# Forgetting attention with two buffer sets per head pair, and the next pair's projections placed among the score steps

## What is computed

```python
def fox_mixer(h, b_f):
    q, k, v, f_logit = jnp.split(h, [MIX_WIDTH, 2 * MIX_WIDTH, 3 * MIX_WIDTH], axis=-1)
    log_f = jax.nn.log_sigmoid((f_logit + b_f).astype(F32))
    decay = jnp.cumsum(log_f, axis=1).transpose(0, 2, 1)
    o = causal_block_attention(split_heads(q, 12), split_heads(k, 12), split_heads(v, 12), decay)
    return merge_heads(o)
# causal_block_attention, for s <= t:
#   logit[t,s] = q_t.k_s/sqrt(dk) + decay[t] - decay[s];  softmax over s;  times v
for i in range(DEPTH):                      # DEPTH = 4, kinds 0, 1, 2, 0
    x = layer_norm(ALPHA * x + 0.5 * swiglu(x, ...), ...)
    h = x @ w_in                            # for kind 0: q | k | v | forget logits | memory q
    main = fox_mixer(h[..., :-MEM_WIDTH], fox_b_f[j])
    mem_out = memory_attention(h[..., -MEM_WIDTH:], mem, mem_w_kv[i])
    x = layer_norm(ALPHA * x + jnp.concatenate([main, mem_out], -1) @ w_o[i], ...)
    x = layer_norm(ALPHA * x + 0.5 * swiglu(x, ...), ...)
```

## Time and profile before

| | us |
|---|---|
| median of six runs | 7801.82 (7759.95 to 8189.87) |
| the profiled run | 7766.0 |
| its span on the slowest core, core 7 | 7764.5 |
| PE busy | 6061.5 (78% of the span) |
| DVE busy | 3044.7 (39%) |
| ACT busy | 1837.7 (24%) |
| Pool busy | 923.9 (12%) |

### The profile page before, as it was taken

How to read it: one execution, slowest core, us unless ns; L and a number is a source line. 1 busy time by engine, 2 the same in 40 slices (tenths; PEclk the granted TensorE clock), 3 DMA queues, 4 the chain that set the end, 5 groups by cost and what they waited for, 6 DMA issues and landing times.

```text
span 7764.5 us, 85500 instructions; the slowest of 8 cores (7712.3 to 7764.5 us)
## 1 busy us (share of the span) xinstructions
PE 6061.5 (78%) x29076; PEld 2816.6 (36%) x29076; DVE 3044.7 (39%) x3788; ACT 1837.7 (24%) x3124; POOL 923.9 (12%) x1426
## 2 busy tenths in 40 slices
PE   7885887789888658898895466659989966885996
PEld 3342443344434223344442133324434432442442
DVE  1326555422322664223226266661321336555132
ACT  1211443211221102112212033321211213442121
POOL 1110111011111000111110011101111110110110
PEclk9996998999999679999996688889999987888998
DMA  7651001466665114656651200017666540110765
GB/s 125 90 77 12 10 10 21 64 92 80 85 93 78 17 16 63 91 77 90 93 79 13 24 7 6 11 19 94 86 92 87 71 60 7 12 15 14 95 87 103
DMA packets 671506, 440.05 MB, mean 57 GB/s; under 512 B 115024, under 2 KB 659792, under 8 KB 671056
## 3 DMA queue, kind: packets, MB, share of 16 engines
q0 software_dynamic: 649024, 401.02, 40.0%
q1 hardware_dynamic: 22064, 33.57, 1.4%
HBM read 826.51 MB, written 8.39 MB: 108 GB/s over the span
## 4 chain that ended last, share of the span: by engine, by line
PE 52%; DVE 16%; ACT 11%; DMA 10%; issue 7%; POOL 2%; DVEq 0%; ACTq 0%; POOLq 0%; SPq 0%
PE ps L220 51%; ACT arena L232 7%; DMA arena<-ffn_w_down 6%; DVE arena L486 3%; DVE st L256 2%; ACT xres L232 2%; PE ps L224 2%; DVE xres L267 2%; DVE xres L277 2%; POOL arena L465 2%; ACT L232 1%; DMA arena<-ffn_w_gate 1%; DMA arena<-w_o 1%; DVE xres L269 1%; ACT rstd L232 1%
## 5 line engine op out<-in xcount | busy, mean ns | idle before, releaser
L220 PE MATMUL ps<-arena 128*128 128x512 bf16 (+7 forms) x24992 | 5710.3, 379 | 1243.4 <-DVE xres L277 195.4
L220 PEld LDWEIGHTS ps<-arena 128*128 128x128 bf16 (+3 forms) x24992 | 2375.8, 101 | 4161.2 <-issue 2038.7
L232 ACT ACTIVATE arena<-ps 128x512 bf16<-128x512 f32 (+4 forms) x2612 | 1389.5, 566 | 3199.1 <-PE ps L220 3048.3
L385 DVE SCALAR_TENSOR_TENSOR arena<-arena,ps 128x512 bf16<-128x512 f32 x704 | 479.8, 687 | 1777.2 <-PE ps L220 1729.2
L486 DVE RECIPROCAL arena<-ps 64x512 f32<-64x512 f32 x208 | 699.0, 3361 | 565.9 <-PE ps L220 558.9
L277 DVE SCALAR_TENSOR_TENSOR xres<-xres,ps 128x512 f32<-128x512 f32 x384 | 246.3, 683 | 1188.4 <-PE ps L220 1178.0
L232 ACT ACT_TABLE_LOAD x107 | 137.3, 1283 | 1796.4 <-DVE mv L258 1584.5
L217 POOL DMA_DIRECT2D arena<-ffn_w_down x384 | 283.6, 740 | 1345.7 <-PE ps L220 1216.3
L224 PE MATMUL ps<-ident,xres 128*128 128x128 f32 x1536 | 218.5, 309 | 271.8 <-ACT arena L232 138.8
L465 POOL TENSOR_TENSOR arena<-arena,tri 128x128 bf16<-128x128 bf16 x576 | 237.1, 425 | 1577.0 <-ACT arena L232 1574.2
L220 PE MATMUL ps<-ident,tri 128*128 128x256 bf16 x2272 | 412.8, 266 | 0.0
(11 more groups left out here) (79 smaller groups left out, 812.4 us busy)
## 6 DMA issues: line engine op xcount, KB each, us to landing
arena<-ffn_w_down POOLq DMA_DIRECT2D x320, 512.0 KB, 6.8
arena<-ffn_w_gate POOLq DMA_DIRECT2D x176, 512.0 KB, 5.8
arena<-ffn_w_up POOLq DMA_DIRECT2D x176, 512.0 KB, 5.8
arena<-ffn_w_down POOLq DMA_DIRECT2D x64, 256.0 KB, 5.2
arena<-fox_w_in POOLq DMA_DIRECT2D x40, 256.0 KB, 5.3
xres<-x SPq DMA_DIRECT2D x4, 2048.0 KB, 27.4
out<-xres SPq DMA_DIRECT2D x4, 2048.0 KB, 9.1
gb<-ln_g SPq DMA_DIRECT2D x12, 512.0 KB, 4.1
```

The lines of the kernel that those rows point to most:

```text
L220: return sc.emit("pe", lambda e: e.matmul(out, lhsT, rhs, start=start, stop=stop), reads, writes, signal=signal)
L232: return sc.emit("act", lambda e: e.activation(out=out, in_=in_, func=func, **kw), reads, writes)
L385: vop(lambda e, fc=fc, bu=bu, th=th: e.scalar_tensor_tensor(out=aT[:, fc, th * 512:(th + 1) * 512], in0=sil[th][:, :], scalar=0.5, in1=psu ...
```

## The change

The buffers of q, k (with their decay and constant rows) and v exist twice, for even and odd pairs. The loads and projections of a pair become a list of 13 items: one that issues the three weight loads and the twelve decay-row transfers, four q groups, four k groups, four v groups. Pair 0's items run at once as before. For pairs 1 to 5 the list is handed to the attention of the pair before as a `Filler`: at every score step that had a dummy pair, the filler is asked, and on every fifth such step one item is issued in the dummy pair's place. What is left at the end of the second head is flushed there.

To make room, the decay buffer now lies over the odd v buffer, the memory attention's k and v over the even one; the three bf16 decay rows are stacked on partitions 0, 32 and 64 of `pc2`, which takes two further casts into a scratch `ptmp`; the constant rows are set in both buffer sets (eight memsets instead of four, two Pool memsets of v instead of one). The other mixers only get a renamed buffer for the memory attention's q.

```diff
+        class Filler:
+            def __call__(self):
+                self.n += 1
+                if self.items and self.n % self.pace == 0:
+                    self.items.pop(0)()
+                    return True
+                return False
+            def flush(self):
+                while self.items:
+                    self.items.pop(0)()
...
-                    if DUMMY_N and c0 == 0:
+                    did = False
+                    if filler is not None and c0 == 0:
+                        did = filler()
+                    if DUMMY_N and c0 == 0 and not did:
...
+            qa = [[carve(35968 + (2 * p + k) * 2048, 2048, BF16) for k in range(2)] for p in range(2)]
+            ka = [[carve(44160 + (2 * p + k) * 2048, 2048, BF16) for k in range(2)] for p in range(2)]
+            Vaug = [carve(52352 + p * 4096, 4096, BF16, "p (i s e) -> p i s e", i=16, s=2) for p in range(2)]
+            pc2 = carve(63104, 2048, BF16)
+            dec = carve(56448, 4096, F32)
...
             for r in range(3):
-                vop(lambda e, r=r: e.tensor_copy(out=pc[0:12, r, :], in_=dec[0:12, :]), ["dec"], ["pc"])
+                vop(lambda e, r=r: e.tensor_copy(out=pc2[32 * r:32 * r + 12, :], in_=dec[0:12, :]), ["dec"], ["pc"])
                 if r < 2:
+                    vop(lambda e: e.tensor_copy(out=ptmp[0:12, :], in_=dec[0:12, :]), ["dec"], ["ptmp"])
...
+            for p in range(2):
+                for s2 in range(2):
+                    vop(lambda e, p=p, s2=s2: e.memset(qa[p][s2][64:70, :], 1.0), [], [("qa", p, s2)])
+                    vop(lambda e, p=p, s2=s2: e.memset(ka[p][s2][64:70, :], -1.0), [], [("ka", p, s2)])
+                vop(lambda e, p=p: e.memset(Vaug[p][:, :, :, 64:128], 1.0), [], [("Vaug", p)], eng="pool")
...
+            def prep_items(hp):
+                p = hp % 2
+                items = []
+                def loads():
+                    dma("pool", wq[:, :, :], w_in_v[:, :, hp * 128:(hp + 1) * 128], [], ["wq"])
...
+                for tb in range(4):
+                    items.append(proj_item(wq, "wq", qa, "qa", 0.125, tb))
+                for tb in range(4):
+                    items.append(proj_item(wk, "wk", ka, "ka", None, tb))
...
+                for q4 in range(4):
+                    items.append(v_item(q4))
+                return items
+            for it in prep_items(0):
+                it()
             for hp in range(6):
+                fill = Filler(prep_items(hp + 1), 5) if hp + 1 < 6 else None
...
-                    attn_core(qa[s2], ("qa", s2), 0, ka[s2], ("ka", s2), 0, 70,
+                    attn_core(qa[p][s2], ("qa", p, s2), 0, ka[p][s2], ("ka", p, s2), 0, 70,
...
+                if fill is not None:
+                    fill.flush()
```

More of the change, by code:

```diff
@@ L193, in build_program @@
         onesb = sb("onesb", [128, 128], BF16)
-        ARENA = 63488
+        ARENA = 65536
         arena = sb("arena", [128, ARENA], BF16)
@@ L433, in build_program, with __init__ @@
         deferred_norm = []
+        class Filler:
+            def __init__(self, items, pace):
+                self.items = list(items)
+                self.pace = pace
+                self.n = 0
+            def __call__(self):
[7 more added lines that the diff above has]
+                    self.items.pop(0)()
         def flush_norm():
@@ new lines, in fox_phase @@
+            ka = [[carve(44160 + (2 * p + k) * 2048, 2048, BF16) for k in range(2)] for p in range(2)]
+            Vaug = [carve(52352 + p * 4096, 4096, BF16, "p (i s e) -> p i s e", i=16, s=2) for p in range(2)]
+            A["PT"] = [carve(60544 + k * 512, 512, BF16) for k in range(3)]
+            A["rec"] = carve(62080, 1024, F32)
+            pc2 = carve(63104, 2048, BF16)
+            dec = carve(56448, 4096, F32)
+            A["kmT"] = carve(52352, 512, BF16, "p (h m) -> p h m", h=2)
@@ L585, in fox_phase @@
             for r in range(3):
-                vop(lambda e, r=r: e.tensor_copy(out=pc[0:12, r, :], in_=dec[0:12, :]), ["dec"], ["pc"])
+                vop(lambda e, r=r: e.tensor_copy(out=pc2[32 * r:32 * r + 12, :], in_=dec[0:12, :]), ["dec"], ["pc"])
                 if r < 2:
-                    vop(lambda e, r=r: e.tensor_tensor(out=dec[0:12, :], in0=dec[0:12, :], in1=pc[0:12, r, :],
-                                                       op=ALU.subtract), ["dec", "pc"], ["dec"])
-            for s2 in range(2):
-                vop(lambda e, s2=s2: e.memset(qa[s2][64:70, :], 1.0), [], [("qa", s2)])
-                vop(lambda e, s2=s2: e.memset(ka[s2][64:70, :], -1.0), [], [("ka", s2)])
@@ new lines, in prep_items, with proj_item, f, v_item @@
+            def prep_items(hp):
[3 more added lines that the diff above has]
+                    dma("pool", wq[:, :, :], w_in_v[:, :, hp * 128:(hp + 1) * 128], [], ["wq"])
+                    dma("pool", wk[:, :, :], w_in_v[:, :, 768 + hp * 128:768 + (hp + 1) * 128], [], ["wk"])
+                    dma("pool", wv[:, :, :], w_in_v[:, :, 1536 + hp * 128:1536 + (hp + 1) * 128], [], ["wv"])
+                    for s2 in range(2):
+                        h = 2 * hp + s2
+                        for r in range(3):
+                            dma("sp", qa[p][s2][64 + r:65 + r, :], pc2[32 * r + h:32 * r + h + 1, :], ["pc"], [("qa", p, s2)])
+                            dma("sp", ka[p][s2][67 + r:68 + r, :], pc2[32 * r + h:32 * r + h + 1, :], ["pc"], [("ka", p, s2)])
+                items.append(loads)
+                def proj_item(w, wkey, dst, dkey, scale, tb):
+                    def f():
+                        b = 5 + (tb % 2)
+                        for c in range(8):
+                            mm(psum[b][:, :], w[:, c, :], xT[:, c, tb * 512:(tb + 1) * 512], c == 0, c == 7,
+                               [wkey, ("xT", c, tb)], [PK(b)], signal=(c == 7))
+                        for s2 in range(2):
+                            dve_copy(dst[p][s2][0:64, tb * 512:(tb + 1) * 512], psum[b][s2 * 64:(s2 + 1) * 64, :], [PK(b)],
+                                     [(dkey, p, s2)], scale=scale)
+                    return f
+                for tb in range(4):
+                    items.append(proj_item(wq, "wq", qa, "qa", 0.125, tb))
+                for tb in range(4):
+                    items.append(proj_item(wk, "wk", ka, "ka", None, tb))
+                def v_item(q4):
+                    def f():
+                        b = 5 + (q4 % 2)
+                        for tl in range(4):
+                            i = 4 * q4 + tl
+                            for c in range(8):
+                                mm(psum[b][:, tl * 128:(tl + 1) * 128], xT[:, c, i * 128:(i + 1) * 128], wv[:, c, :],
+                                   c == 0, c == 7, ["wv", ("xT", c, q4)], [PK(b)], signal=(c == 7 and tl == 3))
+                        dve_copy(Vaug[p][:, 4 * q4:4 * q4 + 4, :, 0:64],
+                                 psum[b][:, :].rearrange("p (i s e) -> p i s e", i=4, s=2), [PK(b)], [("Vaug", p)])
+                    return f
+                for q4 in range(4):
+                    items.append(v_item(q4))
+                return items
@@ L616, in fox_phase @@
[L616 to L619 removed]
+                    attn_core(qa[p][s2], ("qa", p, s2), 0, ka[p][s2], ("ka", p, s2), 0, 70,
+                              lambda kb, p=p, s2=s2: Vaug[p][:, kb, s2, :], ("Vaug", p), lambda tb: 4 * tb + 4, True,
                               lambda tb, h=h: mixT[(h % 2) * 64:(h % 2) * 64 + 64, h // 2, tb * 512:(tb + 1) * 512],
[L621 removed]
+                              lambda tb, h=h: ("mixT", h // 2, tb), A["PT"], A["rec"], filler=fill)
```

78 lines of the change are left out of this document (25 added, 53 removed).

## The result

The changed kernel takes 0.9917 of the time before, with a 95% interval of 0.9882 to 0.9951: 0.5% to 1.2% faster, on both sides of the 1% that the prediction took as its bound. Its profiled run took 7702.7 us, the one before 7766.0; 7694 was predicted, in a range of 7655 to 7765.

What follows compares the result with a forecast made beforehand. PE was taken to bound the attention's long runs of score steps. Removed stages -282.7, items and border waits +197 and set-up +13.6 gave -72 us: 7766 - 72 = 7694 us, range 7655 to 7765.

Steps and rivals of the forecast that it cites:

- Removed: Ten stages between head pairs, five a layer, in which ACT does nothing, disappear: 282.7 us together.
- Items: Projection pieces between attention score steps add to PE's queue almost in full: q and k 12.5 us a pair, v 3.2.
- The refilling rival: After each item the score, exp, PV chain refills at 0.59 us, 59 us for 100 items: 7753 us; chance 0.14.
- the case counted with it: Inside the attention, items wait on DVE's copies through shared banks, so the old stage returns; counted within refilling's 0.14.
- Set-up: Ahead of pair 0, extra DVE casts and memsets delay PE's start by 6.8 us a layer, 13.6 in all.
- The border wait: Between pairs, the first PV waits for the last v copy, queued behind DVE's last normalisation: 0.6 us a pair.
- I leave dips as they are: Dips to 1.2 GHz inside the attention follow waits around the small first block and were taken as unchanged.
- Two signs of being wrong: Granted clock in the pairs leaving 0.89 to 0.94; the stretch of a query block growing by more than its items.
- Little else: For projections between score steps, the change saves the load wait, the cold start, some dummies and little else.
- The greater gain: In the attention, a denser queue ends the clock dips, 17 us and 20 more: 7657 us; chance 0.17.
- The slower case: In the ten filled attention stretches, dips grow; granted share 0.84 uses up the gain, 0.75 gives 7873 us; chance 0.07.
- the Trainium skill's limiter: Three cores of a die on dense matmuls drop to 13/16 clock; the change would lose about 80 us.

## Why the prediction was right

Its sum was -282.7 + 197 + 13.6 = -72; the stretches give -69, the profiled run -63, the ratio -38 to -92. The bounds that it names add up to 7674 to 7735, not to 7670 to 7730.

*Removed.* 5 x 28.4 = 142.0 us a layer, as its 282.7 for both.

*Items.* In the first head five items stand (load, four q), predicted at 4 x 1.56 - 0.16 = 6.1 us; pair 0, which has no border ahead of it, grew by 5.8 there. In the second head stand four k and two v items, predicted 9.5; pairs 1 to 4 grew by 9.3 (pair 0, 8.4). The flush is 3.5 where 3.6 was predicted. The refilling rival would have added 0.59 us an item, 9 us for the first head, and is out. So is the case counted with it, that items wait for DVE's copies. PE's waits over the attention of layer 0, core 5 (before, on core 7: 54.7 us for Pool and 21.9 for weights):

```profile
PE ps L220 <- POOL arena L485: 56.7, 86, 1.7
PE ps L220 <- ACT arena L232: 1.1, 1, 1.1
```

Here too the five border waits are put down to Pool. For weights PE waited twice in the whole kernel, at pair 0 of each layer, 53.5 us together, as the view of this tensor says:

```profile
who waited for it (us, times):
  PE ps L220: 53.5, 2
```

*Set-up.* 6.7 us a layer for 6.8 predicted. From the start of the set-up the first q copy comes 53.8 us later (predicted 779.1 - 724.9 = 54.2, by the row of before above), PE's restart 55.4 us (55.7), the first q groups 44.8 us (45.3).

*The border wait, the step that was mis-sized.* Predicted 0.6 us a pair. The wait itself grew by 0.71. But the first head of pairs 1 to 4 grew by 7.2 us where the items make 6.1, and that of pair 5, which has no items at all, by 1.9: a border costs 1.1 to 1.9 us. What was left out stands behind "I leave dips as they are". Before, PE ran at 1.2 GHz for 92.8 us of a layer's attention, 35.0 of them in the five stages. After, it is 71.0, nearly all inside the pairs, which had 57.8: the time in the stages went with them, as predicted, but 12.8 us came back in the pairs, as in the 6.7 us at 0.50 in the stretch from 879.80, and no term has these. Five borders at 1.1 to 1.9 against 0.6 are 2.5 to 6.5 us a layer; the other terms being slightly cheap, 1.7 of it are left in the sum (41.2 for 42.9). What sets these dips stays open. The longer wait alone does not: with the wait back at 1.0 to 1.1 us on average, PE runs at 1.2 GHz in the first 12 us of a pair for 3.5, 4.1 and 4.9 us in three profiles, and for 6.3 where nothing is flushed, against 5.0 and 5.1 in the two of the changed kernel.

*Signs.* The period of a filled pair is 77.2 us for pair 0 and 78.9 for the next four, in the predicted 77 to 80. Two signs of being wrong did appear: the granted clock of a pair lies between 0.86 and 0.98 over all cores, beyond the 0.89 to 0.94 named on both sides (means 0.91 to 0.95 in filled pairs, 0.88 in pair 5), and first heads grew by more than their items, by the 1.1 to 1.9 us above.

*"Little else".* Right for the size, since PE pays almost all of the projections' 21.6 us again. The runs show what the profile of before did not: of the 28.4 us 3.5 go with the early loads, about 3.3 are DVE's queue at the border and the small transfers behind it, and placing the items is worth 2.0 to 2.5, of which 1.8 are dropped dummies.

*Clock rivals.* The greater gain needed the dips to end, which they did not. The slower case needed 0.84 or less over a filled period; 0.91 was granted over the layer shown. By the Trainium skill's limiter (page TensorE: Matmul & The Clock Gate, section Seeing it yourself) this denser work should have gone to 13/16; in the profiled run of the changed kernel all eight cores show 1.0 and 0.5 alone. The level itself occurs, a third one beside the two named at the start, here 0.81 on core 4 with the normalisation put off, in a feed-forward stretch:

```profile
7195.00:7385.00 190.00, 188.76 (x712) 78.66 (x725) 30.27 (x44) 27.40 (x45) 21.86 (x26) 0.81 0.57 73
```

That kernel interleaves nothing, and the stretch is one that no edit touches; so the prediction's sentence that dense work on all cores has 1.00 is too wide, but the level comes without the change as well.

*Size.* 7702.7 for 7694: of the 9 us, 3 are the border, and the rest is in the part of the span that the change does not touch.

## What to carry to other kernels

Work moved into the slots of a busy engine is paid there almost in full, so cost an interleaving by the waits it removes and by what it replaces; here early loads, second buffers and the order of copies at the border make up 31 of the 41 us a layer when they are taken first, and dropped dummies most of the rest. Before interleaving by hand, try those alone, and look what the last flushed piece stands behind on the copying engine. Compare means of two kernels only together with their granted clock: 5 us of apparent gain of the second buffers were dips. Where new constant rows are needed, set them where that engine waits anyway: it cut the price of the set-up from 6.7 us to 2.7.

## What was not expected of the hardware

At the same border, six small transfers on SP take 7.72 us beside three weight loads and 5.20 without them. Exps of 128 x 512, 0.60 us each, overlap: they can start 0.49 us apart, so a row in which ACT is busy without a gap is no sign that ACT is the bound. And a change that takes 35.0 us at 1.2 GHz out of a layer, in five stages, gets back 12.8 of them inside the pairs that stay: the granted clock of the attention rises only from 0.906 to 0.922.
